# First-key one-hots of odd groups on GpSimd, six value rows summed in the spread stretch

## The reference, cut to what matters

```python
def chunk(zc):                                   # 128 tokens
    ...
    expert = jnp.take_along_axis(cand_idx, top_pos, axis=-1)   # i1 * 128 + i2
    gate = jax.nn.softmax(top_s, axis=-1)
    u = jnp.take(peer_u, expert, axis=0)
    act = jax.nn.gelu(jnp.einsum('chkd,cd->chk', u, zc))
    v = jnp.take(peer_v, expert, axis=0)
    w = (gate * act.astype(jnp.float32)).astype(zc.dtype)
    return jnp.einsum('chk,chkd->cd', w, v).astype(zc.dtype)
```

## Time and profile before

| | us |
|---|---|
| Median of 3 runs | 2670.93 |
| Lowest and highest run | 2669.49, 2675.18 |
| Span of the profiled execution | 2671.2 |
| Spread stretch, first one-hot matmul to first dense matmul | 2227.07 to 2281.67 |
| Dense stretch, to the first use of its sums | 2281.67 to 2659.10 |

### The profile page before, as it was taken

The page is one execution under the profiler, slowest core; times in us unless marked ns, Lnnn a source line. Parts: engine busy times, 40 slices in busy tenths (PEclk is TensorE's granted clock), DMA queues, the critical chain, the costliest instruction groups (busy, mean ns, idle before and its releaser), DMA issues.

```text
span 2671.2 us, 32182 instructions
## 1 busy us (share of the span) xinstructions
PE 2250.8 (84%) x11476; PEld 1809.5 (68%) x11476; DVE 2099.3 (79%) x2971; ACT 1146.8 (43%) x1721; POOL 639.4 (24%) x834
## 2 busy tenths in 40 slices
PE   8999989999999999989999964444555558999997
PEld 7997778888888888879888841111222225777776
DVE  6986647665566556578766999989999999999997
ACT  5433554443444344453542110000355444548876
POOL 1000000000000000000001353542444442786663
PEclk9999999999999999999999976555677778999999
DMA  6534344555555555545558999999999995899996
GB/s 226 179 129 110 111 157 158 188 189 188 189 188 188 185 186 183 168 128 173 165 167 343 422 420 419 420 419 420 419 417 409 420 418 208 347 405 409 409 409 271
DMA packets 314517, 732.02 MB, mean 274 GB/s; under 512 B 21040, under 2 KB 223024, under 8 KB 275760
## 3 DMA queue, kind: packets, MB, share of 16 engines
q0 software_dynamic: 73728, 402.69, 37.1%
q1 hardware_dynamic: 240544, 327.03, 35.9%
q10 hardware_dynamic: 144, 1.05, 0.1%
HBM read 728.61 MB, written 2.10 MB: 274 GB/s over the span
## 4 chain that ended last, share of the span: by engine, by line
DVE 23%; PE 17%; DMA 13%; issue 3%; POOL 2%; ACT 1%; DVEq 0%; SPq 0%; ACTq 0%; PEldq 0%; POOLq 0%
DVE row L2497 12%; DMA row<-in_peer_u,expert 8%; DMA row<-in_peer_v_rows,expert 5%; PE pg L1294 4%; PE pl L865 4%; PE pl L872 3%; DVE pl L2513 2%; POOL row L801 1%; PE pl L868 1%; PE pl L869 1%; DMA v_tile<-in_peer_v_dense 1%; PE pg L1285 1%; PE pl L1259 1%; PE pl L1188 1%; POOL spread_lo L776 1%
## 5 line engine op out<-in xcount | busy, mean ns | idle before, releaser
L1957 DVE TENSOR_TENSOR wlo<-raw,whi 128x1024 fp32r<-128x1024 f32 (+1 forms) x436 | 517.9, 1208 | 374.9 <-ACT whi L1341 373.3
L1341 ACT ACTIVATE whi<-raw 128x1024 fp32r<-128x1024 f32 (+1 forms) x436 | 444.6, 1039 | 412.0 <-PE pl L872 407.2
L2497 DVE CUSTOM_DVE_ANT_0 row<-row,pg 128x2048 f32<-128x2048 f32 x256 | 574.7, 2284 | 34.0 <-DMA row<-in_peer_u,expert 32.3
L1259 PE MATMUL pl<-row,diag 128*128 128x512 f32 x404 | 316.7, 930 | 333.6 <-DMA row<-in_peer_v_rows,expert 297.8
L865 PE MATMUL pl<-x_split,whi 128*128 128x512 f32 x1888 | 478.5, 395 | 10.2 <-DVE x_split L1965 5.3
L1259 PEld LDWEIGHTS pl<-row,diag 128*128 128x128 f32 x404 | 101.1, 276 | 500.2 <-issue 445.2
L865 PEld LDWEIGHTS pl<-x_split,whi 128*128 128x128 f32 x1888 | 341.5, 190 | 74.6 <-issue 7.5
L872 PE MATMUL pl<-x_split,wlo 128*128 128x256 f32 x2656 | 373.7, 284 | 3.9 <-DVE wlo L1957 3.9
L872 PEld LDWEIGHTS pl<-x_split,wlo 128*128 128x128 f32 x2656 | 359.0, 192 | 23.1 <-DVE wlo L1957 4.5
L801 POOL DMA_INDIRECT row<-in_peer_u,expert x256 | 242.8, 949 | 367.1 <-DVE dots L2497 155.7
L801 POOL DMA_INDIRECT row<-in_peer_v_rows,expert x256 | 261.4, 1021 | 199.4 <-DVE dots L2497 67.0
(11 more groups left out here) (348 smaller groups left out, 3041.6 us busy)
## 6 DMA issues: line engine op xcount, KB each, us to landing
v_tile<-in_peer_v_dense SPq DMA_DIRECT2D x128, 512.0 KB
raw<-in_w_in SPq DMA_DIRECT2D x51, 1024.0 KB
raw<-in_w_gate SPq DMA_DIRECT2D x44, 1024.0 KB
raw<-in_w_up SPq DMA_DIRECT2D x44, 1024.0 KB
raw<-in_w_out SPq DMA_DIRECT2D x32, 1024.0 KB
raw<-in_w_down SPq DMA_DIRECT2D x32, 1024.0 KB
wq<-in_peer_wq SPq DMA_DIRECT2D x15, 1024.0 KB, 11.5
raw<-in_w_down SPq DMA_DIRECT2D x16, 768.0 KB
```

Of the source, the lines that this page charges most:

```text
L1259: last = mm(pl_all[:, c:c + width], diag[:, (at - 1) % 4, :], row[b][:, c - DENSE:c - DENSE + width], start=at == 1, stop=at == ADDED_ROWS ...
L1341: return nc.scalar.activation(o, i, ACT.Copy)
L1957: V.tensor_tensor(wlo[:, n % 4, 0:k, :], w[:, :, f, :], whi[:, n % 4, 0:k, :].bitcast(F32), ALU.subtract)\
L2497: V.tensor_tensor_reduce(row[b][:], row[b][:], z_tok[:], 1.0, 0.0, ALU.mult, ALU.add, dots[:, at:at + 1])\
```

## The change

GpSimd makes the first-key one-hots of the odd groups of t = 1, as four instructions of 128 x 128 for each group (VectorE made them in one of 128 x 512). VectorE makes those of the even groups as before, and all second-key one-hots. Six value rows of t = 1 (the first six) move in the order from behind the 27 rows of t = 0 to among the last 14 rows that TensorE adds: VectorE sums one of them after each of the groups 5, 10, 15, 21, 26 and 31. So 149 rows instead of 155 are left for the dense stretch, where `rows_by` spreads them over the same 122 tiles. `PAUSE_ROWS` lists, for the 14 and the 6 rows, the group behind which each is used; GpSimd's queue takes its one-hots for groups up to four past that group ahead of the fetch that waits for the row. TensorE waits for one more semaphore in odd groups (`keys_ready`).

```diff
+def pause_rows():
+    adds = [(after_group(a, ADDED_ROWS - EARLY), 0, EARLY + a) for a in range(ADDED_ROWS - EARLY)]
+    sums = [(after_group(a, PAUSE_SUMS), 1, HROWS + a) for a in range(PAUSE_SUMS)]
+    return sorted(adds + sums)
...
-    return order + sums[taken:]
+    paused = [at for _, _, at in PAUSE_ROWS]
+    return order + [sums[at] for at in paused] + [w for at, w in enumerate(sums) if at >= taken and at not in paused]
...
-SUMMED_ROWS = PRODUCTS - ADDED_ROWS
+SUMMED_ROWS = PRODUCTS - ADDED_ROWS - PAUSE_SUMS
...
+            def first_keys(g):
+                n = GROUPS + g
+                if g == 1:
+                    pool.wait_ge(turned_ready, 2)
+                pool.wait_ge(hot_used, n - HOTS + 1)
+                for c in range(GROUP):
+                    token = g * GROUP + c
+                    last = nc.gpsimd.tensor_scalar(hot_a[n % HOTS][:, c, :], iota[:], turned[:, 0, token:token + 1], None, ALU.is_equal)
+                last.then_inc(keys_ready, 1)
...
+                if LATER + PAUSE_HOMES <= j < ADDED_END + PAUSE_HOMES:
+                    while keyed < min(GROUPS, PAUSE_ROWS[j - LATER - PAUSE_HOMES][0] + HOTS + 1):
+                        first_keys(keyed)
+                        keyed += 2
...
                 if t == 0:
                     pe.wait_ge(first_ready, FIRST_READY + 3 * n + 3)
+                elif g % 2:
+                    pe.wait_ge(keys_ready, KEYS_READY + g // 2 + 1)
...
-                if t:
+                if t and g % 2 == 0:
                     V.tensor_tensor(a[:], iota[:].unsqueeze(1).broadcast_to(full),
                                     wide(turned[:, 0, g * GROUP:(g + 1) * GROUP], 2, full), ALU.is_equal)
...
             for g in range(GROUPS):
                 hot_group(1, g)
+                for after, t, at in PAUSE_ROWS:
+                    if t and after == g:
+                        sum_row(t, *divmod(at - HROWS, TOPK))
```

More of the change, by code:

```diff
@@ L65, with after_group @@
 ADDED_ROWS = 101
+PAUSE_SUMS = 6
 PRODUCTS = TT * HROWS
+GROUP = 4
+GROUPS = P // GROUP
+def after_group(index, count):
+    return -(-(index + 1) * GROUPS // count) - 1
+def pause_rows():
+    adds = [(after_group(a, ADDED_ROWS - EARLY), 0, EARLY + a) for a in range(ADDED_ROWS - EARLY)]
+    sums = [(after_group(a, PAUSE_SUMS), 1, HROWS + a) for a in range(PAUSE_SUMS)]
+    return sorted(adds + sums)
+PAUSE_ROWS = pause_rows()
 def row_order():
@@ L96 @@
 LATER = PRODUCTS + EARLY
-ADDED_END = PRODUCTS + ADDED_ROWS
-SUMMED_ROWS = PRODUCTS - ADDED_ROWS
+ADDED_END = PRODUCTS + ADDED_ROWS + PAUSE_SUMS
+SUMMED_ROWS = PRODUCTS - ADDED_ROWS - PAUSE_SUMS
+PAUSE_ADDED = [what for what in ROW_ORDER[LATER:ADDED_END] if row_user(*what) == "add"]
 ROWS_AT = {0: range(2), 2: range(2, 4), 8: range(4, 6), 20: range(6, 7), 24: range(7, 9), 31: range(9, 11), 37: range(11, 13),
@@ L137, in rows_by @@
     return min(SUMMED_ROWS, (m + 1) * SUMMED_ROWS // (NKEY - 6))
-GROUP = 4
-GROUPS = P // GROUP
 TURNED = TOPK * (PH + 1)
@@ L527, in build @@
         FIRST_READY = 4
+        keys_ready, KEYS_READY = q0_done, 1
+        PAUSE_HOMES = len(ROWS_AT[LATER])
         def landed(unit):
@@ L777, in low_weights @@
                     .then_inc(spread_low, 1)
-            low = 0
+            def first_keys(g):
[7 more added lines that the diff above has]
+                last.then_inc(keys_ready, 1)
+            low, keyed = 0, 1
             for j, (table, t, n, k) in enumerate(ROW_ORDER):
+                if LATER + PAUSE_HOMES <= j < ADDED_END + PAUSE_HOMES:
+                    while keyed < min(GROUPS, PAUSE_ROWS[j - LATER - PAUSE_HOMES][0] + HOTS + 1):
+                        first_keys(keyed)
+                        keyed += 2
                 while j >= ADDED_END and rows_by(low + 1) < j - ADDED_END:
@@ L1327, in _ @@
                 if (g + 1) * added // GROUPS > g * added // GROUPS:
-                    add_row(*ROW_ORDER[LATER + g * added // GROUPS][1:])
+                    add_row(*PAUSE_ADDED[g * added // GROUPS][1:])
             pe.wait_ge(spread_ready, TT * GROUPS)
@@ L1876, in _ @@
             for j in range(2):
-                weight_matrix(*ROW_ORDER[LATER + j][1:])
+                weight_matrix(*PAUSE_ADDED[j][1:])
             turned_copy(1)
@@ L1882, in _ @@
                 if (g + 1) * added // GROUPS > at and at + 2 < added:
-                    weight_matrix(*ROW_ORDER[LATER + at + 2][1:])
+                    weight_matrix(*PAUSE_ADDED[at + 2][1:])
                 if g == GROUPS - 2:
@@ L2515, in add_sums @@
             def add_sums(t):
-                dve.wait_ge(row_summed, SUMMED_ROWS if t else HROWS - ADDED_ROWS)
+                dve.wait_ge(row_summed, PRODUCTS - ADDED_ROWS if t else HROWS - ADDED_ROWS + PAUSE_SUMS)
                 a = acc[:, t, DENSE:]
```

## The result

The changed kernel is slower: 2677.69 us median of 6 runs (2673.20 to 2682.05) against 2671.05 (2669.40 to 2675.18) for the kernel before, ratio 1.0024 with a 95% interval of 1.0014 to 1.0034. The forecast was 2664.4 with a range of 2662 to 2674. The profiled execution has a span of 2675.8 us and a time of 2677.93.

The account below looks back on a forecast made before the run. It took TensorE, with VectorE nearly as tight, to bound the spread stretch and DMA, TensorE close behind, the dense one. Dense stretch -6.5 and spread stretch 0, from the median of 2670.9, gave 2664.4 us, range 2662 to 2674.

Parts of the forecast that it names:

- GpSimd's first keys: Spread stretch: a GpSimd one-hot priced like a select of its size, 0.295 us, 1.18 a group, so in time.
- upper bound of 0.32 from the two-input row: GpSimd's one-hot: a two-input 128 x 512 instruction takes 1.295 us, or 0.32 for each 128 columns.
- The sum around the price: GpSimd's queue, spread stretch: 1.18 us a set plus 1.43 for fetches, 2.61, under the 3.29 TensorE needs.
- GpSimd is late: Rival, chance 0.10: stretched GpSimd one-hots lengthen the spread stretch by 8.7 us, to 2673.1, or by 12.8, to 2677.2.
- case of 2.66 us a set: Spread stretch: GpSimd's one-hots at the two-input rate and also stretched lengthen it by 12.8 us, to 2677.2.
- The threshold of 1.86 us a set: Spread stretch: above 3.29 - 1.43 = 1.86 us a set of GpSimd one-hots would no longer come in time.
- Six rows fewer in the dense stretch: Dense stretch: less DMA work gains 6.5 us, between 5.6 and the full 7.7.
- The first three groups: Start of the spread stretch: 4.70 us because VectorE delivers a group in 1.63; 0.6 earlier possible, counted as 0.
- Six sums on VectorE: Spread stretch: they add 7.2 us to VectorE, hidden only if it keeps ahead of TensorE.
- The shared use of SBUF: Spread stretch: half of 64 GpSimd instructions hit VectorE for 0.14 us each, 4.5 us; at most 18.9.
- VectorE is blocked: Rival, chance 0.22: GpSimd's reads block VectorE in the spread stretch; 9.5 us gives 2668.8, the full 18.9 gives 2678.2.
- sign named for GpSimd's lateness: Profile after, spread stretch: TensorE waiting for `hot_a` from GpSimd, with a longer stretch.

Follow-up runs that it names:

- e5_forms: The kernel before with eleven more GpSimd instructions at its start, into memory that nothing reads; 2674.16 us in one run.
- f1_short_keys: The changed kernel with each GpSimd one-hot written for 32 of 128 columns only; 2669.79 us, ratio 0.9993 to the kernel before.
- f2_drop_six: The kernel before without the last six value rows of the second 128 tokens, neither fetched nor summed; 2663.48 us, ratio 0.9960.
- e2_keys_only: The changed kernel with GpSimd's first keys kept but no value row moved; 2681.04 us, ratio 1.0034 to the kernel before.
- e3_sums_only: The changed kernel with the six sums moved but all first keys made by VectorE; 2670.05 us, ratio 0.9997 to the kernel before.

## Why the prediction was wrong, point by point

- **GpSimd's first keys: the step that failed.** "I take 0.295, so 1.18 us a group." The nearest row by engine and size was a different operation. Alone, the one-hot takes 0.600 us, and in the changed kernel a set of four took 41.3/15.5 = 2.66. The upper bound of 0.32 from the two-input row failed as well, for it too was another operation, and it divided a long instruction by four. That leaves out what each instruction costs whatever its length, for the comparison 0.350 - 32 x 0.0026 = 0.27 us by e5_forms; for the two-input instruction no run shows it. The sum around the price was sound: 18 fetches for 15.5 sets make 1.47 us a set (19.1 us busy and 3.7 idle), 2.66 + 1.47 = 4.13 against 3.29, and 16 x 0.84 = 13.4 us, where 13.3 were measured, 12.5 if the slower start is left out. The rival "GpSimd is late" held, down to its case of 2.66 us a set, for which it named 12.8 us and 2677.2; its mechanism was a stretched instruction, though, and what was measured is mostly a slow one. That its price met the measured one, and its time the median of 2677.69, is luck: two wrong factors made the 2.66, and the dense stretch gave 4.0 in place of 6.5.
- **The threshold of 1.86 us a set.** It is an average, and its other term was a little low: in f1_short_keys the fetches cost 1.53 us a set and not 1.43, so a set of 1.75 came just to the 3.29 that TensorE takes. TensorE lost 2.6 us to GpSimd there, at sets behind two fetches in a row.
- **Six rows fewer in the dense stretch: -6.5.** Right in size without GpSimd's sets (7.0 and 7.8); 4.0 and 6.2 in two executions of the changed kernel.
- **The first three groups.** The prediction put their 4.70 us down to VectorE's 1.63 us a group. The granted clock of 0.50 was the other bound: in f2_drop_six, with the same instructions on VectorE, they took 5.44, and in the changed kernel, where VectorE leaves out the first keys of group 1, 5.49. Of the 0.6 us that the prediction saw there and left out of its sum, 0.1 shows (4.57 in e2_keys_only and f1_short_keys).
- **Six sums on VectorE, hidden only if it keeps ahead.** Shown: 5.2 us lost when it keeps its first keys. In the changed kernel they are hidden, under GpSimd's lateness.
- **The shared use of SBUF: 4.5 us.** About right in size, by luck in its terms. VectorE's instructions in the stretch, in the kernel before and in the changed one:

```profile
L2542 DVE TENSOR_SCALAR hot_b<-iota,turned 128x128 f32<-128x128 f32 x128 | 36.2, 351 | 0.0
L2534 DVE TENSOR_TENSOR hot_a<-iota,turned 128x512 f32<-128x512 f32 x32 | 22.0, 686 | 2.9 <-ACT turned L1341 2.9
```

```profile
L2583 DVE TENSOR_SCALAR hot_b<-iota,turned 128x128 f32<-128x128 f32 x128 | 39.4, 387 | 2.5 <-PE pg L1326 2.5
L2575 DVE TENSOR_TENSOR hot_a<-iota,turned 128x512 f32<-128x512 f32 x16 | 11.8, 740 | 6.5 <-PE pg L1326 4.2 <-ACT turned L1382 2.2
```

  The second keys are 3.2 us longer in all, and sixteen first keys 0.05 each, 0.9: 4.1 us of busy time for 64 instructions of GpSimd. Without GpSimd's keys, in e3_sums_only and e5_forms, the second keys came to 36.0 and 36.2 us, as before. The prediction had 32 hits of 0.14; measured are 0.064 for each of 64, and each was more than twice as long as reckoned, so the share of its length was 0.1 and not 0.24. The rival "VectorE is blocked" fails. The rule of the Trainium skill, "SBUF — State Buffer", section "Who interferes with whom", that of two instructions which need the shared ports the later blocks fully, shows here at most in part: with 41.3 us of one-hots on GpSimd and 51.2 on VectorE in 67.6 us the two ran beside each other for much of the time, and VectorE lost 4.1 us, not 43. Whether VectorE's second keys need the shared ports at all, no run tells.
- **Where it would show.** The sign named for GpSimd's lateness, TensorE waiting for `hot_a`, is there, but under the name of `hot_b` or "issue".

## What to carry to other kernels

Price an instruction on another engine by that instruction: a few copies of it where both engines are idle show its price, and here they settled the question that a neighbouring row of the same size had answered wrongly by a factor of two. When work goes to an engine that also issues transfers, add both in its queue and look at the worst place, not at the mean; for nine sets placed where the consumer has other things to do TensorE never waited (the stretch grew by 1.8 us, through VectorE's sums), sixteen at even distance lengthened it by 13.3. And look for the idle engine whose price the trace already holds: ScalarE had made the same one-hots for the first 128 tokens, at 2.0 us a set, and with nine of them, and five rows moved, the kernel became 0.24% faster.

## What the hardware showed that was not expected

- A GpSimd comparison with one number per partition: 0.600 us for 128 x 128 fp32 alone, 0.350 for 128 x 32, 0.53 for 128 x 128 with a constant (partly beside VectorE), while a select of that size takes 0.29.
- Beside VectorE the same instruction took 0.678 us (128 columns, 13% more) and 0.483 (32 columns, 38% more).
- The first three groups of the spread stretch took 4.57 to 5.49 us, with TensorE's granted clock at 0.50 for most of them (before, 2227.5 to 2230.5; changed, 2222.5 to 2227.5).
- The dense stretch of one kernel differs by 2.2 us between two executions (373.39 and 371.20), that of the kernel before's code by 1.7 (377.43 and 379.11), and the start of the spread stretch by 7 us between kernels that are the same up to there.
